# A 1-core f32 transformer pair: GpSimd exchanges halves for the rotary step, modulation rows go through memory, and experts are chosen in three groups of tiles with X spilled

## Chip, cores, metric

One Trainium2 chip, one core. The metric is the device time of one execution in microseconds. Three runs of the kernel before took 1822.27, 1818.64 and 1820.02 us: median 1820.02. The profiled execution took 1820.39 us; its first to last instruction, the span, is 1819.1 us.

## What is computed

Two transformer blocks in f32 on 512 tokens of width 1024. The first block is a hybrid mixer (differential attention with rotary queries and keys beside an mLSTM), a cross attention over 256 memory rows, and a mixture of 32 experts; the second runs two layers of a convolution beside a sparse attention, each behind a modulated norm. What the change touches, cut from the reference:

```python
def rotary(t, pos):                       # per head of 64: halves of 32
    t1, t2 = t[..., : d // 2], t[..., d // 2:]
    return jnp.concatenate([t1 * cos - t2 * sin, t2 * cos + t1 * sin], axis=-1)

x = x + cross_attention(rms_norm(x, norm_x_g), rms_norm(mem, norm_mem_g), w_xq, w_xk, w_xv, w_xo)
x = x + hierarchical_moe(rms_norm(x, norm_ffn_g), w_rg, b_rg, w_re, b_re, w1, w3, w2)
# in hierarchical_moe
g_idx = jnp.argmax(softmax(xt @ w_rg + b_rg))                 # one of 4 groups
e_logits = (xt @ w_re + b_re) of that group                   # 8 experts, the best 2 are taken
y = (silu(x_blk @ w1[e]) * (x_blk @ w3[e])) @ w2[e]           # rows sorted by expert
# in the second block, for each of two layers
mod = silu(c) @ w_ada[l] + b_ada[l]; shift, scale, gate = split(mod, 3)
h = rmsnorm(x, g_pre[l]) * (1 + scale) + shift
```

## The kernel before

Every engine runs its own program, written out by hand in the order of its work. `Count.step` adds to a semaphore when an instruction ends, `done` gives the value to wait for. The kernel is walked twice, once to number the steps and once to build. PSUM is eight banks of 128 x 512, handed out in turn by `Banks.take`: TensorE waits for whoever last read the bank. SBUF is one arena. Weights of 2 MB each go through ring slots (`Ring`): SP issues a load when the last reader of its slot is done (`ends`; the issue is line 164), so the order of loads and the time at which slots come free set the weight stream. `product` (line 185, its matmul is line 187) is the helper through which nearly all products go; each 128x128 by 128x512 f32 product of one chunk is two matmul instructions, so a product over 8 chunks is sixteen.

**Input stage** (`pe_mixer_in`, `act_mixer_in`, `dve_mixer_in`). For each of 8 groups g of queries and keys TensorE makes a product "qk"; ACT copies it to `raw[g % 2]`; TensorE multiplies `raw` by a permutation matrix (`pe_swap`, line 614), which exchanges the halves of 32 within each 64 partitions; DVE multiplies the exchanged rows by a signed sine (line 1249), `raw` by the cosine (1250), and adds them (1252). `raw` is free again when the rotation two groups back is done. Between rotations DVE sums w_ada's rows weighted by silu(c) into `macc` (`dve_ada`, lines 1211 and 1214: one multiplication and seven multiply-adds of 512 columns for each half). When both halves of a part (shift or scale) are in, TensorE sums over the partitions (`pe_mod`, line 576): eight products of 128x128 by a column of ones, so that the 1024 sums stand as [128, 8], and DVE adds the bias (`dve_mod`). For layer 0 the two sums stand behind "qk" 4 and 6. Then come four value products, and attention. For layer 1 the two sums stand in the output projection of the mixer, behind its fourth and its last tile, ahead of the transposes of the normalised rows for cross attention.

**Router** (`pe_router`, `act_router`, `dve_router`). The last projection w_xo is made in eight products of tile t and half n. For each of four tiles DVE adds it to X (line 1460), ACT sums squares, GpSimd takes the root (line 1763), DVE makes the normalised row times the gain (`dve_put_f`, line 1494), ACT stores the row to memory (`h3_rows`), and TensorE transposes it (line 801). Logits are made for two tiles at a time, turned back to tokens (821), and picked on DVE (`dve_router_pick`, lines 1555 to 1589: a chain of some 20 small operations); ranks, places and the table of slots follow (`dve_router_place`, lines 1600 to 1605, and 1631 to 1634). With the table GpSimd gathers the rows of each expert by indirect DMA (line 1776), once h3 is all stored.

**Experts.** 32 experts with w1, w3 and w2 of 2 MB each, 96 loads in the order w1.0 w3.0 w1.1 w3.1 w2.0 w1.2 w3.2 w2.1 ... (w2 of an expert follows w1 and w3 of the next). Nine slots take them in turn; the first ones are loaded while cross attention and router still run, the two that held w_xo when it is done, `features` (HT) when the logits are done, and `router` when slots and stores are done. For each expert TensorE turns 64 gathered rows (875), multiplies by w1 and w3 side by side, turns (898), multiplies by w2; ACT and DVE copy, and GpSimd scatters the result (1784). Behind the experts the scattered rows are read back and added to X (`dve_row_sum`, `pe_row_sum`).

## Time and profile before

| | |
|---|---|
| median of 3 runs | 1820.02 us |
| profiled execution, device time | 1820.39 us |
| its span | 1819.1 us |
| PE busy | 1653.1 us, 91% of the span |
| DVE, ACT, POOL busy | 727.4, 478.0, 317.5 us |
| DMA | 324.30 MB, 178 GB/s over the span |
| expert weights | 96 loads of 2 MB, median 34.7 us from issue to landing |

A line of code named in the profile is a line of the kernel before; a line can be that of a helper. PE is TensorE, PEld its weight loads, DVE VectorE, ACT ScalarE, POOL GpSimd, SP SyncE. PEclk is the granted clock of TensorE, as a share of 2.4 GHz; the DMA share is the mean busy share of the 16 DMA engines. "<-" names what ended an engine's idle time. A row of a timeline that merges instructions ("x88") names the form of the first.

### The profile page before, as it was taken

To read this page: it belongs to the slowest core of one execution; us is meant where nothing else is said; L and a number is where in the kernel's file an instruction comes from. 1 tells how busy PE (TensorE), PEld (TensorE's weight loads), DVE (VectorE), ACT (ScalarE), POOL (GpSimd) and SP (SyncE) were. 2 spreads that over 40 slices of the span, in tenths; PEclk is the share of its full clock that TensorE was granted. 3 is DMA by queue.
4 is the path that set the end of the run, shared out by engine and by line. 5 is a ranking of instruction groups with operands and counts; after the bars stand their busy time and mean duration, and the time that the engine had idled before them with its cause. 6 is when DMAs were issued, how large, how long until landed. Compare 5 with 4: busy or idle time off the path is not lost.

```text
span 1819.1 us, 15312 instructions
## 1 busy us (share of the span) xinstructions
PE 1653.1 (91%) x5832; PEld 814.8 (45%) x5832; DVE 727.4 (40%) x1519; ACT 478.0 (26%) x979; POOL 317.5 (17%) x312
## 2 busy tenths in 40 slices
PE   6999999999989699898887787999989999998898
PEld 3544446645454333333333333444455554445553
DVE  2626634254152312111100111459875143996622
ACT  2013242101130010000000001566365134645631
POOL 0000000000000112111101100148143012742500
PEclk9899999999999799898898998989999999899999
DMA  8321032356262599999999998401102130020101
GB/s 322 139 93 46 1 116 93 139 185 236 69 248 87 220 365 408 407 401 409 402 399 403 407 415 325 178 1 70 69 1 88 46 110 0 7 109 24 47 1 46
DMA packets 70960, 324.30 MB, mean 178 GB/s; under 512 B 9290, under 2 KB 12626, under 8 KB 58464
## 3 DMA queue, kind: packets, MB, share of 16 engines
q1 hardware_dynamic: 63552, 308.03, 43.6%
q0 software_dynamic: 6016, 10.51, 1.8%
q10 hardware_dynamic: 1312, 4.72, 0.7%
q8 instruction: 48, 0.79, 0.2%
q14 instruction: 32, 0.26, 0.0%
HBM read 318.95 MB, written 12.67 MB: 182 GB/s over the span
## 4 chain that ended last, share of the span: by engine, by line
PE 68%; DMA 19%; DVE 9%; ACT 2%; issue 2%; POOL 0%; SPq 0%; ACTq 0%; DVEq 0%; POOLq 0%
PE bank L187 65%; DMA arena<-in_w 15%; DMA arena<-h_rows,arena 3%; DVE arena L2454 1%; DVE arena L1214 1%; DVE arena L2438 1%; PE bank L2053 1%; PE bank L567 1%; DVE arena L2495 1%; DVE arena L2508 0%; PE bank L875 0%; DMA arena<-in_params 0%; PE bank L2000 0%; PE bank L662 0%; DVE bank L2486 0%
## 5 line engine op out<-in xcount | busy, mean ns | idle before, releaser
L187 PE MATMUL bank<-arena 128*128 128x512 f32 (+11 forms) x4964 | 1548.0, 551 | 90.6 <-DMA arena<-in_w 53.2
L187 PEld LDWEIGHTS bank<-arena 128*128 128x128 f32 (+3 forms) x4964 | 710.4, 181 | 858.9 <-issue 789.5
L2669 POOL TENSOR_TENSOR arena<-arena 128x512 f32<-128x512 f32 x180 | 205.4, 1141 | 224.1 <-ACT arena L2279 206.6
L1763 POOL TENSOR_TENSOR arena<-arena 128x1 f32<-128x1 f32 (+2 forms) x44 | 32.4, 738 | 682.3 <-DVE arena L1204 456.9
L1711 DVE TENSOR_TENSOR arena<-arena,bank 64x512 f32<-64x512 f32 x32 | 22.1, 691 | 314.2 <-ACT arena L1170 314.2
L2279 ACT ACTIVATE arena<-arena 128x512 f32<-128x512 f32 x180 | 125.9, 717 | 19.6 <-POOL arena L2669 19.3
L959 ACT COPY arena<-bank 128x512 f32<-128x512 f32 (+3 forms) x114 | 60.8, 540 | 228.4 <-PE bank L187 147.3
L1170 ACT ACTIVATE arena<-bank 64x512 f32<-64x512 f32 x32 | 18.9, 591 | 379.6 <-PE bank L187 379.6
L1784 POOL DMA_INDIRECT y_rows<-arena x32 | 32.1, 1004 | 413.4 <-PE bank L875 272.6
L1705 DVE COPY arena<-bank 128x512 f32<-128x512 f32 x32 | 22.1, 692 | 115.2 <-PE bank L875 115.2
L1214 DVE SCALAR_TENSOR_TENSOR arena<-arena 128x512 f32<-128x512 f32 x84 | 63.2, 752 | 3.0
L2466 DVE MAX8 arena<-arena 128x8 f32<-128x512 f32 (+2 forms) x96 | 54.1, 563 | 3.3
L2438 DVE SCALAR_TENSOR_TENSOR arena<-arena 128x512 f32<-128x512 f32 x60 | 54.6, 910 | 0.9
L875 PE MATMUL bank<-arena 64*128 64x64 f32 x256 | 35.0, 281 | 22.0 <-DMA arena<-h_rows,arena 22.0
L2053 PE MATMUL bank<-arena 128*128 128x128 f32 x160 | 27.2, 290 | 27.6 <-DVE arena L2508 19.4
L2468 DVE MATCH_REPLACE8 arena<-arena 128x512 f32<-128x512 f32 (+2 forms) x96 | 52.2, 544 | 0.0
L875 PEld LDWEIGHTS bank<-arena 64*128 64x128 f32 x256 | 30.6, 200 | 47.0 <-DMA arena<-h_rows,arena 30.8
L2454 DVE SCALAR_TENSOR_TENSOR arena<-arena 128x512 f32<-128x512 f32 (+2 forms) x42 | 42.7, 1017 | 4.5 <-ACT arena L2226 0.2
L2241 ACT ACTIVATE arena<-arena 128x128 f32<-128x128 f32 (+3 forms) x64 | 35.5, 555 | 33.8 <-DVE arena L2495 23.3
L2486 DVE TENSOR_TENSOR bank<-bank,arena 128x256 f32<-128x256 f32 (+1 forms) x44 | 22.0, 499 | 55.7 <-PE bank L187 55.6
L1180 ACT COPY arena<-bank 128x512 f32<-128x512 f32 x32 | 18.8, 586 | 92.4 <-PE bank L187 92.4
L2053 PEld LDWEIGHTS bank<-arena 128*128 128x128 f32 x160 | 18.7, 145 | 51.3 <-DVE arena L2508 33.6
(264 smaller groups left out, 876.6 us busy)
## 6 DMA issues: line engine op xcount, KB each, us to landing
arena<-in_w SPq DMA_DIRECT2D x96, 2048.0 KB, 34.7
arena<-in_w_in SPq DMA_DIRECT2D x15, 2048.0 KB, 10.8
arena<-in_w_ada SPq DMA_DIRECT2D x12, 2048.0 KB, 8.7
arena<-in_w_out SPq DMA_DIRECT2D x6, 2048.0 KB, 7.7
arena<-in_w_xk SPq DMA_DIRECT2D x2, 2048.0 KB, 9.3
arena<-in_w_xv SPq DMA_DIRECT2D x2, 2048.0 KB, 8.6
arena<-in_w_xq SPq DMA_DIRECT2D x2, 2048.0 KB, 9.9
arena<-in_w_xo SPq DMA_DIRECT2D x2, 2048.0 KB, 9.1
```

Source lines behind the costliest of these rows:

```text
L187: i = pe.e.matmul(o, l, r, start=first and j == 0, stop=last and j == len(pairs) - 1)
L875: i = pe.e.transpose(b[:, c * BLK:(c + 1) * BLK], xg[:, c, :], k.ident[0:BLK, 0:BLK])
L959: act.e.copy(dst, src).then_inc(*k.act.step(*name))
L1214: dve.e.scalar_tensor_tensor(out=acc, in0=w[:, c, :], scalar=k.CACT[:, c:c + 1], in1=acc, op0=ALU.mult, op1=ALU.add).then_inc(*(k.dve.step ...
L2053: i = pe.e.transpose(b[:, c * 128:(c + 1) * 128], k.tmp[s % 4][:, c * 128:(c + 1) * 128], k.ident)
L2241: i = act.e.activation(e, e, ACT.Exp, scale=-1.0 if g == 1 else 1.0, bias=ds[:, j:j + 1], accum_out=ds[:, 4 + j:5 + j])
L2279: act.e.activation(k.prod[l][n % 4], x, ACT.Identity, scale=w, bias=0.0).then_inc(*k.act.step("prod", l, f, j))
L2438: dve.e.scalar_tensor_tensor(out=yc, in0=x, scalar=cw, in1=yc, op0=ALU.mult, op1=ALU.add).then_inc(*V.step("tap", l, f, j))
L2454: dve.e.scalar_tensor_tensor(out=S, in0=r, scalar=w, in1=S, op0=ALU.mult, op1=ALU.add).then_inc(*V.step("is", l, n))
L2466: dve.e.max(m8, S).then_inc(*V.step())
L2468: dve.e.match_replace(S, m8, S, TAKEN).then_inc(*V.step())
L2669: pool.e.tensor_tensor(yc, yc, k.prod[l][n % 4], ALU.add).then_inc(*k.pool.step("sum", l, f, j))
```

## The change

1. *Exchange on GpSimd.* `pe_swap` and its matrix go. Behind ACT's copy of group g, GpSimd makes four multiplications of 32 partitions by 512, each reading one quadrant of `raw` and of the sine (its rows exchanged beforehand) and writing the neighbouring quadrant of `rt[g % 2]`. DVE's sine multiplication goes; it waits for GpSimd, multiplies by the cosine and adds.
2. *Shift and scale as rows.* The sum over partitions is now a product of a column of ones by 256 columns of `macc`, four of them into partitions 0, 32, 64 and 96 of the bank. DVE copies it to `mrow`, ACT issues four stores to memory, GpSimd one load that brings it back as [128, 8]; bias, 1 and gain are put in by DVE ahead of the experts.
3. *Router.* Tiles are chosen in groups (0, 1), (2), (3). TensorE transposes X itself, by chunks of 128 columns, half a tile at a time; the gain is multiplied into the router's weights, the root into the logits. Logits of two chunks are made side by side in 64 columns each and added in the turn back. Tile 3 of the last projection is split in halves, with the router's steps of the first groups between. The stored row is X times its root, made by ACT; the gain is multiplied in when an expert's rows are copied.
4. *X in memory.* ACT stores X, its 2 MB of SBUF become a tenth slot, and SP loads X back behind the last expert weight. SP waits for the last stored row ahead of w3 of expert 2, and for both first gathers ahead of w2 of expert 1.

The diff, cut to its core:

```diff
-        slots = [i * 4096 for i in range(SLOTS)] + [base + 5876, base + 9972, ht_at, base + 14068]
+        slots = [i * 4096 for i in range(SLOTS)] + [base + 5876, base + 9972, ht_at, base + 14068, x_at]
...
-    R.ends[features] = [(P, ("lg", 1))]
+    R.ends[features] = [(P, ("lg", 2))]
     R.ends[router] = [(P, ("slot",)), (k.h3_out[0], ("h3", 2)), (k.h3_out[1], ("h3", 3))]
-    R.go_on([ring[2], ring[3], tokens, cross, ring[4], ring[0], ring[1], features, router])
+    R.ends[residual] = [(k.x_out, ("x", 3)), (k.act, ("sq", "f", 3)), (k.act, ("xn", "f", 3)), (P, ("tr", 3, 1))]
+    R.go_on([ring[2], ring[3], tokens, cross, ring[4], ring[0], ring[1], features, residual, router])
     def expert(name, e, c, n, end):
         R.load(sp, (name, e), k.a[name][e].rearrange("(p c) n -> p c n", c=c), (c, n), P, (end, e))
...
     for e in range(NE + 1):
         if e < NE:
             expert("w1", e, 8, 512, "up")
+            if e == 2:
+                sp.wait_ge(*k.h3_out[1].done("h3", 3))
             expert("w3", e, 8, 512, "up")
+            if e == 2:
+                for j in range(2):
+                    sp.wait_ge(*k.xg_in[j].done(j))
             if e == 0:
                 sp.wait_ge(*P.done("xs", 7))
-                sp.e.dma_start(k.WR, rows(k.a["w_router"], 8, 40)).then_inc(*k.wr_in.step("w"))
+                sp.e.dma_start(k.WR, chunks(k.a["w_router"], 8)).then_inc(*k.wr_in.step("w"))
         if e:
             expert("w2", e - 1, 4, 1024, "dn")
+    for c, n in R.ends[residual]:
+        sp.wait_ge(*c.done(*n))
+    sp.e.dma_start(k.X, k.x_d.rearrange("(t p) d -> p t d", p=128)).then_inc(*k.x_back.step("x"))
...
-    acc = k.macc.rearrange("p (q k) -> p k q", k=8)
     pe.wait_ge(*k.dve.done("ada", l, part, 1))
-    for c in range(8):
-        i = product(pe, b[:, c:c + 1], [(acc[:, c, :], k.C("ones", 0, 1))])
+    for n in range(4):
+        i = product(pe, b[32 * n:32 * n + 1, 0:256], [(k.C("ones", 0, 1), k.macc[:, n * 256:(n + 1) * 256])])
     i.then_inc(*k.pe.step("mod", l, part))
...
-        if g:
-            pe_swap(k, pe, g - 1)
...
-def pe_swap(k, pe, g):
-    b = k.banks.take(pe, k.dve, "swap", g)
-    pe.wait_ge(*k.act.done("qk", g))
-    product(pe, b, [(k.C("swap"), k.raw[g % 2])]).then_inc(*k.pe.step("swap", g))
...
+GROUPS = ((0, 1), (2,), (3,))
+def pe_router_turn(k, pe, t, halves=(0, 1)):
+    for q in halves:
         b = k.banks.take(pe, k.dve if q else k.act, "tr", t, q, among=ROUTER_BANKS)
-        pe.wait_ge(*k.dve.done("xn", "f", t))
+        pe.wait_ge(*k.dve.done("o", "w_xo", t, q))
         for f in range(4):
-            i = pe.e.transpose(b[:, f * 128:(f + 1) * 128],
-                               k.XNf[t % 2].rearrange("p (q k) -> p k q", k=8)[:, 4 * q + f, :], k.ident)
+            i = pe.e.transpose(b[:, f * 128:(f + 1) * 128], k.X[:, t, q * 512 + f * 128:q * 512 + f * 128 + 128], k.ident)
         i.then_inc(*k.pe.step("tr", t, q))
-def pe_router_logits(k, pe, u):
-
-    w = k.WR
-    pe.wait_ge(*k.wr_in.done("w"))
-    b = k.banks.take(pe, k.act, "lg", u, among=ROUTER_BANKS)
-    for t in (2 * u, 2 * u + 1):
-        pe.wait_ge(*k.act.done("tr", t, 0))
-        pe.wait_ge(*k.dve.done("tr", t, 1))
-    product(pe, b[0:40, 0:256], [(w[:, c, :], k.HT[:, c, u * 256:u * 256 + 256]) for c in range(8)]).then_inc(*k.pe.step("lg", u))
+def pe_router_out(k, pe, t, n, half):
+    b = k.banks.at("o", "w_xo", t, n) if half else k.banks.take(pe, k.dve, "o", "w_xo", t, n, among=ROUTER_BANKS)
+    w = k.ring.at(("w_xo", half), 4, 1024)
+    i = product(pe, b, [(k.OT[:, 4 * half + c, t * 128:(t + 1) * 128], w[:, c, n * 512:(n + 1) * 512]) for c in range(4)],
+                not half, bool(half))
+    if half:
+        i.then_inc(*k.pe.step("o", "w_xo", t, n))
+def pe_router_logits(k, pe, u, pairs, first=True, last=True):
+    t, end = GROUPS[u][0], GROUPS[u][-1] + 1
+    cols = slice(t * 128, end * 128)
+    n = (end - t) * 128
+    pe.wait_ge(*k.dve.done("wr"))
+    b = k.banks.take(pe, k.act, "lg", u, among=ROUTER_BANKS) if first else k.banks.at("lg", u)
+    for j, pair in enumerate(pairs):
+        for m, c in enumerate(pair):
+            pe.wait_ge(*(k.act.done("tr", end - 1, 0) if c < 4 else k.dve.done("tr", end - 1, 1)))
+            i = product(pe, b[64 * m:64 * m + 64, 0:n], [(k.WR[:, c, :], k.HT[:, c, cols])],
+                        first and j == 0, last and j == len(pairs) - 1)
+    if last:
+        i.then_inc(*k.pe.step("lg", u))
...
-    pe_out(k, pe, "w_xo", k.OT, [(2, 1), (3, 0)])
+    pe_out(k, pe, "w_xo", k.OT, [(2, 1)])
+    pe_router_logits(k, pe, 0, [(c, c + 4) for c in range(4)])
+    pe_router_out(k, pe, 3, 0, 0)
+    pe_router_tokens(k, pe, 0)
     pe_router_turn(k, pe, 2)
-    pe_out(k, pe, "w_xo", k.OT, [(3, 1)])
-    pe_router_logits(k, pe, 0)
-    pe_router_tokens(k, pe, 0)
-    pe_router_turn(k, pe, 3)
-    pe_router_logits(k, pe, 1)
+    pe_router_out(k, pe, 3, 0, 1)
+    pe_router_ranks(k, pe, 0)
+    pe_router_logits(k, pe, 1, [(c, c + 4) for c in range(4)])
+    pe_router_out(k, pe, 3, 1, 0)
     pe_router_tokens(k, pe, 1)
-    pe_router_ranks(k, pe, 0)
+    pe_router_turn(k, pe, 3, (0,))
+    pe_router_out(k, pe, 3, 1, 1)
     pe_router_slots(k, pe, 0)
     pe_router_ranks(k, pe, 1)
+    pe_router_logits(k, pe, 2, [(0, 1), (2, 3)], True, False)
+    pe_router_turn(k, pe, 3, (1,))
+    pe_router_logits(k, pe, 2, [(4, 5), (6, 7)], False, True)
+    pe_router_tokens(k, pe, 2)
     pe_router_slots(k, pe, 1)
+    pe_router_ranks(k, pe, 2)
+    pe_router_slots(k, pe, 2)
...
+        if g in (5, 7):
+            act_mod(k, act, 0, g // 2 - 2)
...
+    act.wait_ge(*k.pool.done("root", "f", t))
+    act.e.activation(k.XNf[t % 2], k.X[:, t, :], ACT.Copy, scale=k.f_ss[:, t:t + 1]).then_inc(*k.act.step("xn", "f", t))
+    act.wait_ge(*k.act.last())
     act.e.dma_start(k.h3_d[t * 128:(t + 1) * 128, :], k.XNf[t % 2]).then_inc(*k.h3_out[t % 2].step("h3", t))
+def act_router_squares(k, act, t):
+    act.wait_ge(*k.dve.done("o", "w_xo", t, 1))
+    if t >= 2:
+        act.wait_ge(*k.h3_out[t % 2].done("h3", t - 2))
+    act.e.activation(k.XNf[t % 2], k.X[:, t, :], ACT.Square, accum_out=k.f_ss[:, t:t + 1]).then_inc(*k.act.step("sq", "f", t))
...
+    for t in range(3):
+        act_router_squares(k, act, t)
+        if t == 2:
+            act_router_logits(k, act, 0)
+        act_router_turn(k, act, t)
+        act_x_store(k, act, t)
+        act_row_store(k, act, t)
+    act_router_logits(k, act, 1)
     act_router_turn(k, act, 3)
-    act_router_logits(k, act, 1)
+    act_router_squares(k, act, 3)
+    act_router_logits(k, act, 2)
+    act_row_store(k, act, 3)
+    act_x_store(k, act, 3)
...
+    if (l, part) != (0, 0):
+        dve.wait_ge(*k.mod_out.done((2 * l + part - 1) // 2, (part + 1) % 2, 3))
     dve.wait_ge(*k.pe.done("mod", l, part))
-    if part == 0:
-        dve.e.tensor_tensor(dst, b[:, 0:8], k.P(f"bshift{l}"), ALU.add).then_inc(*V.step("mod", l, part))
-    else:
-        dve.e.tensor_tensor(dst, b[:, 0:8], k.P(f"bscale{l}"), ALU.add).then_inc(*V.step("mod", l, part))
-        dve.wait_ge(*V.last())
-        dve.e.tensor_scalar(dst, dst, 1.0, None, ALU.add).then_inc(*V.step())
-        dve.wait_ge(*V.last())
-        dve.e.tensor_tensor(dst, dst, k.P(f"gpre{l}"), ALU.mult).then_inc(*V.step("scale", l))
+    dve.e.tensor_copy(k.mrow[0:97, :], k.banks.at("mod", l, part)[0:97, 0:256]).then_inc(*k.dve.step("mod", l, part))
+def act_mod(k, act, l, part):
+    act.wait_ge(*k.dve.done("mod", l, part))
+    for n in range(4):
+        act.e.dma_start(k.mod_d[2 * l + part:2 * l + part + 1, n * 256:(n + 1) * 256],
+                        k.mrow[32 * n:32 * n + 1, :]).then_inc(*k.mod_out.step(l, part, n))
+def pool_mod(k, pool, l, part):
+    pool.wait_ge(*k.mod_out.done(l, part, 3))
+    pool.e.dma_start(k.MOD[:, 2 * l + part, :], k.mod_d[2 * l + part].rearrange("(p k) -> p k", k=8)).then_inc(
+        *k.mod_in.step(l, part))
+def dve_mod_end(k, dve, l):
+    V, shift, scale = k.dve, k.MOD[:, 2 * l, :], k.MOD[:, 2 * l + 1, :]
+    dve.wait_ge(*k.mod_in.done(l, 1))
+    dve.e.tensor_tensor(shift, shift, k.P(f"bshift{l}"), ALU.add).then_inc(*V.step("shift", l))
+    dve.e.tensor_tensor(scale, scale, k.P(f"bscale{l}"), ALU.add).then_inc(*V.step())
+    dve.wait_ge(*V.last())
+    dve.e.tensor_scalar(scale, scale, 1.0, None, ALU.add).then_inc(*V.step())
...
-        dve.wait_ge(*P.done("swap", g))
-        dve.e.tensor_tensor(tmp, B.at("swap", g), C("sin"), ALU.mult).then_inc(*V.step("swap", g))
+        dve.wait_ge(*k.pool.done("swap", g))
         dve.e.tensor_tensor(raw, raw, C("cos"), ALU.mult).then_inc(*V.step())
         dve.wait_ge(*V.last())
...
+def pool_swap(k, pool, g):
+    raw, tmp = k.raw[g % 2], k.rt[g % 2]
+    pool.wait_ge(*k.act.done("qk", g))
+    if g >= 2:
+        pool.wait_ge(*k.dve.done("rot", g - 2))
+    for q in range(4):
+        src, dst = slice(32 * q, 32 * q + 32), slice(32 * (q ^ 1), 32 * (q ^ 1) + 32)
+        i = pool.e.tensor_tensor(tmp[dst, :], raw[src, :], k.C("sin")[src, :], ALU.mult)
+    i.then_inc(*k.pool.step("swap", g))
...
+    for t in range(3):
         dve_add_out(k, dve, "w_xo", t)
         dve_mean_square(k, dve, k.f_ss[:, t:t + 1], D, "f", t)
-        if t == 2:
-            dve_gate(k, dve, 1, 1)
-        dve_put_f(k, dve, t)
-        if t < 3:
+        if t < 2:
             dve_router_turn(k, dve, t)
+    dve_gate(k, dve, 1, 1)
     dve.e.memset(k.TAB, 2 * T).then_inc(*V.step("tab"))
-    dve_router_pick(k, dve, 0, lambda: dve_router_turn(k, dve, 3))
+    dve_router_pick(k, dve, 0, lambda: dve_router_turn(k, dve, 2))
+    dve_add_half(k, dve, "w_xo", 3, 0)
     dve_router_place(k, dve, 0)
     dve_router_pick(k, dve, 1)
+    dve_add_half(k, dve, "w_xo", 3, 1)
+    dve_router_turn(k, dve, 3)
+    dve_mean_square(k, dve, k.f_ss[:, 3:4], D, "f", 3)
     dve_router_place(k, dve, 1)
+    dve_router_pick(k, dve, 2)
+    dve_router_place(k, dve, 2)
...
-    dve.e.tensor_copy(k.xt[e % 2], B.at("xT", e).rearrange("p (k s) -> p k s", k=8)).then_inc(*V.step("xT", e))
+    dve.e.tensor_tensor(k.xt[e % 2], B.at("xT", e).rearrange("p (k s) -> p k s", k=8),
+                        k.P("gffn").unsqueeze(2).broadcast_to([128, 8, BLK]), ALU.mult).then_inc(*V.step("xT", e))
...
+    pool.wait_ge(*k.c2_in.done("consts"))
+    for g in range(8):
+        pool_swap(k, pool, g)
+    for part in range(2):
+        pool_mod(k, pool, 0, part)
```

## Rows read from the trace of the kernel before

**Rows 1.** The page: PE busy time, and the chain by engine

```profile
PE 1653.1 (91%) x5832; PEld 814.8 (45%) x5832; DVE 727.4 (40%) x1519; ACT 478.0 (26%) x979; POOL 317.5 (17%) x312
...
PE 68%; DMA 19%; DVE 9%; ACT 2%; issue 2%; POOL 0%; SPq 0%; ACTq 0%; DVEq 0%; POOLq 0%
```

**Rows 2.** Busy us (x instructions), PEclk, DMA share and GB/s by stage

```profile
0.00:123.00 123.00, 108.55 (x272) 53.72 (x272) 47.15 (x78) 15.48 (x24) 2.39 (x8) 0.96 0.51 187
...
598.00:642.00 44.00, 26.68 (x128) 15.20 (x126) 16.70 (x71) 5.50 (x9) 6.19 (x7) 0.77 0.63 232
642.00:1107.00 465.00, 398.25 (x1796) 161.24 (x1796) 58.62 (x122) 37.52 (x64) 64.94 (x66) 0.90 1.01 406
```

**Rows 3.** Timeline of the input stage: start us, us, engine, line, instructions

```profile
20.09 38.08 PE L187 MATMUL bank<-arena 128*128 128x512 f32 x88 [0.89 <-ACT arena L952]
58.54 22.62 PE L187 MATMUL bank<-arena 128*128 128x1 f32 x52 [0.37 <-DVE arena L1214]
81.44 57.79 PE L187 MATMUL bank<-arena 128*128 128x1 f32 x160 [0.28 <-DVE arena L1214]
...
123.31 0.58 ACT L959 COPY arena<-bank 128x512 f32<-128x512 f32 x1 [13.15 <-PE bank L187]
```

**Rows 4.** Window right behind the second summing product of the input stage

```profile
85.50:89.00 3.50, 3.50 (x5) 1.37 (x5) 0.45 (x3) 0.00 (x0) 0.00 (x0) 0.52 0.00 0
```

**Rows 5.** Groups: gate product, DVE accumulation and rotation, GpSimd addition (its ns min/median/max)

```profile
L187 PE MATMUL bank<-arena 128*4 128x512 f32 x32 | 7.0, 591 | 0.0
...
L1214 DVE SCALAR_TENSOR_TENSOR arena<-arena 128x512 f32<-128x512 f32 x84 | 63.2, 752 | 3.0
...
L1252 DVE TENSOR_TENSOR arena<-arena 128x512 f32<-128x512 f32 x8 | 5.5, 694 | 0.3
...
L2669 POOL TENSOR_TENSOR arena<-arena x180: 1087/1090/1570, 1198.4 to 1724.7; 128x512 f32<-128x512 f32 x180
```

**Rows 6.** Timeline of DVE and GpSimd where both run at once

```profile
1203.33 8.48 DVE L2454 SCALAR_TENSOR_TENSOR arena<-arena 128x512 f32<-128x512 f32 x7
...
1203.65 1.38 POOL L2669 TENSOR_TENSOR arena<-arena 128x512 f32<-128x512 f32 x1 [0.71 <-ACT arena L2279]
...
1208.45 1.09 POOL L2669 TENSOR_TENSOR arena<-arena 128x512 f32<-128x512 f32 x1 [0.43 <-ACT arena L2279]
```

**Rows 7.** Window behind an idle stretch of PE that ended at 509.8 us

```profile
510.00:515.00 5.00, 5.00 (x17) 4.17 (x17) 1.56 (x6) 1.49 (x5) 0.00 (x0) 0.50 1.02 429
```

**Rows 8.** Timeline at the first output projection, and one DMA issue of ACT

```profile
368.88 65.83 PE L187 MATMUL bank<-arena 128*128 128x512 f32 x160 [2.40 <-DVE arena L1452]
...
434.35 0.75 DVE L1485 TENSOR_SCALAR arena<-arena 128x1024 f32<-128x1024 f32 x1 [0.44 <-POOL arena L1763]
...
L1116 ACTq DMA_DIRECT2D h_rows<-arena x4: 326/330/333, 569.4 to 602.8; - x4
```

**Rows 9.** Timeline of the router: one pick of two tiles, slots, gather, landing

```profile
598.80 0.69 DVE L1460 TENSOR_TENSOR arena<-arena,bank 128x512 f32<-128x512 f32 x1 [5.58 <-PE bank L187]
...
611.95 0.23 DVE L1555 TENSOR_TENSOR arena<-bank,arena 128x80 f32<-128x80 f32 x1
...
616.01 0.23 DVE L1581 TENSOR_TENSOR arena<-arena 128x64 f32<-128x64 f32 x1
...
620.79 0.18 DVE L1631 TENSOR_SCALAR arena<-bank 64x32 f32<-64x32 f32 x1 [2.01 <-PE bank L187]
...
622.05 1.04 POOL L1776 DMA_INDIRECT arena<-h_rows,arena  x1 [18.77 <-DVE arena L1634]
...
630.02 2.02 PE L875 MATMUL bank<-arena 64*128 64x64 f32 x16 [7.98 <-DMA arena<-h_rows,arena]
```

**Rows 10.** Windows around the expert stage, and the issues of its weights

```profile
630.00:642.00 12.00, 11.67 (x56) 5.60 (x56) 2.31 (x6) 1.28 (x2) 1.86 (x2) 0.78 0.18 40
...
1120.00:1130.00 10.00, 4.21 (x16) 1.37 (x12) 0.00 (x0) 0.59 (x1) 1.47 (x2) 0.83 0.35 123
...
arena<-in_w SPq DMA_DIRECT2D x96, 2048.0 KB, 34.7
```

183 lines of the change are left out of this document (92 added, 91 removed).

## The prediction

> **What bounds the kernel now.** I read the page first: PE is busy nine tenths of the span and holds 68% of the chain, DMA 19% [rows 1]. Then the windows by stage: up to 598 us PE has little idle time, from 598 to 642 it is idle 17 us, and from 642 to 1107 the DMA share is 1.01 at 406 GB/s [rows 2]. So three things are to be priced: PE's work in the input stage, the latency of the router, and the moment from which the weight stream runs without a gap. Behind 1131 us the change alters nothing that I can price, and I let it stand.
>
> **Input stage, PE.** 88 instructions take 38.08 us, 0.433 each [rows 3], so a product of sixteen takes 6.9 and an exchange product of two 0.87. From 20.1 to the end of the last value product at about 122.7 (ACT copies it at 123.3, rows 3) are 102.6 us: twelve products 83.1, eight exchanges 6.9, and 12.6 for the two sums over partitions (pe_mod). These cost 6.3 each because their sixteen one-column instructions take about 4 and because PE then runs at 1.2 GHz: the granted clock behind the second is 0.52 for 3.5 us [rows 4]. The exchanges go. A sum becomes eight instructions of 256 columns into four column groups; the nearest row is the gate product, 32 instructions of 512 columns in 7.0 us as pairs [rows 5], so 0.11 each for half the columns, 0.9 in all. Bounds: 0.5 if four run at once, 1.7 if none do. I take 1.0. If PE never waited, the stage would end at 20.1 + 83.1 + 2.0 = 105.2, 17.5 sooner.
>
> **Input stage, GpSimd and DVE.** It will wait. The exchange becomes four GpSimd multiplications of 32 partitions and 512 columns. The trace has none of that form; the nearest is the addition of 128 partitions, 1.09 at the median [rows 5], and I take that, since a partition holds as many elements. Bounds: 0.3 (the four side by side) and 1.6 (about the longest of that row, 1.57). DVE loses one of three operations a rotation, and its accumulations for the sums have two SBUF inputs. Seven such took 8.48 us while four GpSimd additions began [rows 6], against 0.752 each alone [rows 5]: 3.2 more, 0.8 for each GpSimd operation. The chain: the second product ends at 34.0, ACT copies it (0.6), GpSimd 4.4, DVE rotates (1.4 with 0.69 an operation, rows 5): 40.4. Two accumulations of 6.0 and one rotation of 1.3 follow before the first sum: 53.7 undisturbed, under PE's own 54.7. But the exchanges of products 2, 3 and 4 fall in there, 12 operations, 9.6 us: 63.4. PE waits 8.7. Then a copy (0.4), two rotations and two accumulations, 15.0, with seven GpSimd operations, 5.6, put the second sum at 84.0, where PE could be at 78.2. One sum, one query or key product and four value products later it is 119.7, 3.0 sooner than before. After such waits the clock drops: in 510 to 515 us, behind 3.7 us of idleness, it was 0.50 [rows 7]. The first drop hides in the wait for the second sum; the second costs about 2. **Gain 1.0.** GpSimd's own queue has nothing else to do meanwhile, the DMA issues of the rows (four on ACT, 0.33 each, one on GpSimd) stand beside PE work, and the rotation of the last key product is done by 98, before attention wants it. The Trainium skill ("SBUF — State Buffer", Within the engine side) says that such a pair holds the port exclusively for the whole instruction: a GpSimd operation would then cost DVE 1.09 and not 0.8, the 19 of them 5.5 us more, and the sum would be 1815. The row shows a part overlapped, and I keep to the row.
>
> **Output projection.** The 160 instructions take 65.83 [rows 8]; 128 are projection, 55.4, so the two sums cost 5.2 each. The first falls to 1.0: 4.2. The second covers DVE's chain to the last normalised tile, which ends at 435.1 [rows 8], four us behind the last projection; without the cover PE waits for it: 0. ACT's four issues, 0.33 each [rows 8], now stand before its first copy of features: up to 1.3 lost, I take 0.5. **Gain 3.7.**
>
> **Router.** Before: the last projection ends 0.6 before DVE's addition at 598.8, slots at 620.8, gather issued 622.05, landed 630.02 [rows 9]. After, on the same clock: transposes of X itself need no root and no gain, and logits, ranks and picks of the first tiles lie between halves of the last projection. They push that one back by 6.7, to 604.9. A pick took 4.1 for two tiles [rows 9], 3.1 for one. Behind the last projection come addition and transposes with the slots of the first group (2.8), copy, logits, copy, turn back (2.3), one pick (3.1), ranks, place, slots and index (2.2): 615.3, and the gather is issued 0.9 later at 616.2, 5.8 sooner. Three small groups instead of two cost DVE one more pick, hidden under the projection. Landing took 8.0 with one weight load in flight; now w3 of expert 2 is in flight, but issued 2 us before, behind the last stored row: 6.4, so 622.6, **7.4 sooner**. Bounds: issue 3 to 8 sooner, landing 4 to 8.
>
> **Weight stream.** Before, from 630 to 642 the DMA share is 0.18, since all nine slots are full until expert 0's first half is done; from 642 on 87 loads take 465 us, 5.35 each [rows 2, 10]. After, SP holds w2 of expert 1 until both gathers have landed. Seven loads are in; 89 remain, of which three have free slots (X's is one), 16 us, longer than expert 0's first half needs. So the stream has no gap from 624.6 on and ends at 624.6 + 476 = 1100.4: **gain 6.8**. The stores of X, 2 MB, lie in the projection's idle DMA time except the last. X comes back behind the last weight: 2.1 MB, 5.2 us at the stream's rate; from 1120 to 1130 the DMA share is 0.35 [rows 10], which hides it, but the last scatter meets it: 0 to 5, I take **1.0 lost**. Eight small DVE operations for shift and scale, about 1.6, and the gain multiplied in at each expert's copy hide under expert 0's weights.
>
> **Sum.** 1.0 + 3.7 + 6.8 − 1.0 = 10.5. The profiled execution is 1820.4 (span 1819.1), 0.4 above the median: **1810**.
>
> **Rivals.**
> (B) The four GpSimd multiplications run side by side, a swap taking some 1.3 instead of 4.4. Then DVE meets the first sum in time, PE waits 3 at the second, and the stage ends at 108.0, 14.7 sooner and not 1.0: 1796. For it: they use different partitions and nothing waits between them. Against: no row shows GpSimd operations overlapping. The Trainium skill ("GPSIMD Engine Reference", the note on consecutive Pool instructions) has each core go on to the next instruction once its own 16 partitions are done, which is this case. Chance 0.27.
> (C) The gather lands no sooner, because GpSimd also waits for the last stored row, whose store stands last on ACT. Then the stream starts at 632 and ends 0.6 later than before, plus 1.0 for X: 1817. For it: ACT does the scaled copy only after the last logits. Against: that copy ends at 611, five us before the gather's issue. Chance 0.10.
> (D) Slower: reading one quadrant and writing another makes the multiplication dearer. At 1.6 with the same overlap, 19 of them hold DVE back 9.7 more, and two exchanges that stand alone ahead of a rotation 2 each; the stage ends some 13.5 later than forecast: 1823. It decides from about 1.5 an operation. For it: the form is in no row. Against: the element count is that of the 1.09 row. Chance 0.10.
> The forecast has 0.50; 0.03 is left for what I have not seen.
>
> **How the numbers follow.** A measurement of this kernel can tell about 0.2%, 3.6 us, from no change. Forecast and B lie below 1816.4, C about on the bound (half of it same), D above. Faster 0.82, same 0.08, slower 0.10. The forecast's own range is 1803 to 1816 by its bounds; with B the range reaches down to 1792, and up to 1819 for C; D and the rest, 0.13, are outside.
>
> **What would show it.** Value products ending near 122 with PE idle before both sums (forecast) or near 108 without the first (B); GpSimd multiplications of 1.1 us in a row, not at once; DVE's accumulations there at up to 1.5 us instead of 0.75; no clock drop behind the sums themselves. In the router a gather issued 11 us behind the last projection and not 24, and no gap of the DMA share between the gather's landing and the last weight. The forecast is wrong in its largest term if the accumulations stay at 0.75, and in its second if the stream has a gap or ends less than 480 us behind the landing.

## The result, and the profile after

The changed kernel took 1807.16 us (median of 5 runs, 1802.55 to 1809.38) beside 1819.09 us before (5 runs, 1817.05 to 1822.27): ratio 0.9931, 95% interval 0.9917 to 0.9944, so it is faster by more than the noise. The forecast was 1810, with a range of 1803 to 1816. The profiled execution is the one of 1807.16 us, with a span of 1805.8, 13.3 less than in the profile before.

The page of the changed kernel: busy time, the chain by engine, and the groups of DVE's accumulations and GpSimd's multiplications (busy us, mean ns, idle before):

```profile
PE 1629.6 (90%) x5808; PEld 795.6 (44%) x5808; DVE 738.5 (41%) x1525; ACT 483.4 (27%) x984; POOL 366.5 (20%) x348
...
PE 66%; DMA 20%; DVE 10%; ACT 2%; issue 1%; POOL 1%; DVEq 0%; ACTq 0%; POOLq 0%; SPq 0%
...
L1264 DVE SCALAR_TENSOR_TENSOR arena<-arena 128x512 f32<-128x512 f32 x84 | 78.4, 934 | 3.0
...
L1349 POOL TENSOR_TENSOR arena<-arena 32x512 f32<-32x512 f32 x32 | 46.4, 1449 | 41.5 <-ACT arena L999 38.5
```

The windows by stage of the changed kernel, columns as in [rows 2]:

```profile
0.00:123.00 123.00, 94.04 (x244) 43.05 (x244) 60.64 (x68) 15.75 (x25) 50.08 (x42) 0.94 0.51 187
598.00:642.00 44.00, 32.60 (x176) 17.25 (x176) 13.81 (x56) 8.39 (x12) 6.76 (x8) 0.81 0.88 337
642.00:1107.00 465.00, 401.39 (x1788) 163.55 (x1786) 57.37 (x120) 35.37 (x60) 64.81 (x67) 0.90 1.00 405
```

PE is 14.5 us less busy in the first stage and the stage is as long as before. Between 598 and 642 us the DMA share is 0.88 where it was 0.63 [rows 2].

To see where the 13.3 us come from, one takes the same events in both timelines. Five of the kernel before that [rows 3, 8, 9] do not hold: the first product of cross attention, of w_xo, of expert 31, the last product of expert 31, and the first product of the second block.

```profile
442.11 64.03 PE L187 MATMUL bank<-arena 128*128 128x512 f32 x164 [0.15 <-issue]
...
540.05 20.84 PE L187 MATMUL bank<-arena 128*128 128x512 f32 x48 [0.87 <-DVE arena L1502]
...
1107.57 10.54 PE L187 MATMUL bank<-arena 128*64 128x512 f32 x48 [2.46 <-DMA arena<-in_w]
...
1119.33 3.65 PE L187 MATMUL bank<-arena 128*64 128x512 f32 x16 [0.61 <-DVE arena L1719]
1127.75 1.22 PE L187 MATMUL bank<-arena 128*128 128x256 f32 x2 [4.76 <-issue]
```

The timeline of the changed kernel behind the input stage: the output projection with PE's waits behind it, the same events, DVE's last addition of the projection w_xo, and the gather:

```profile
373.53 56.48 PE L187 MATMUL bank<-arena 128*128 128x512 f32 x144 [2.40 <-DVE arena L1532]
...
432.29 0.38 PE L581 MATMUL bank<-arena 128*128 128x128 f32 x1 [1.85 <-DVE arena L1569]
433.48 5.33 PE L581 MATMUL bank<-arena 128*128 128x128 f32 x29 [0.82 <-DVE arena L1569]
...
439.71 64.02 PE L187 MATMUL bank<-arena 128*128 128x512 f32 x164 [0.15 <-issue]
...
534.77 20.84 PE L187 MATMUL bank<-arena 128*128 128x512 f32 x48 [0.87 <-DVE arena L1576]
...
599.35 0.69 DVE L1539 TENSOR_TENSOR arena<-arena,bank 128x512 f32<-128x512 f32 x1 [0.45 <-PE bank L187]
...
611.47 1.04 POOL L1864 DMA_INDIRECT arena<-h_rows,arena  x1 [6.52 <-DVE arena L1719]
...
617.04 2.02 PE L906 MATMUL bank<-arena 64*128 64x64 f32 x16 [5.58 <-DMA arena<-h_rows,arena]
...
1094.58 10.54 PE L187 MATMUL bank<-arena 128*64 128x512 f32 x48 [2.59 <-DMA arena<-in_w]
...
1106.35 3.65 PE L187 MATMUL bank<-arena 128*64 128x512 f32 x16 [0.61 <-DVE arena L1805]
1115.45 7.68 PE L187 MATMUL bank<-arena 128*128 128x256 f32 x20 [5.45 <-issue]
```

| event | before | after | gained on the way there |
|---|---|---|---|
| ACT copies the last value tile | 123.31 | 122.73 | 0.6 |
| output projection begins | 368.88 | 373.53 | −5.2 |
| cross attention begins | 442.11 | 439.71 | 7.1 |
| w_xo begins | 540.05 | 534.77 | 2.9 |
| the gathered rows have landed | 630.02 | 617.04 | 7.7 |
| last product of expert 31 | 1119.33 | 1106.35 | 0.0 |
| second block begins | 1127.75 | 1115.45 | −0.7 |
| end of the span | 1819.1 | 1805.8 | 1.0 |

**Input stage.** The changed kernel's timeline there (PE's products; GpSimd's exchanges of the first and the third group; DVE's seven multiply-adds of each half; ACT's last copy):

```profile
20.03 34.64 PE L187 MATMUL bank<-arena 128*128 128x512 f32 x80 [0.89 <-ACT arena L983]
65.61 16.03 PE L187 MATMUL bank<-arena 128*1 128x256 f32 x40 [10.94 <-DVE arena L1264]
86.06 39.31 PE L187 MATMUL bank<-arena 128*1 128x256 f32 x102 [4.42 <-DVE arena L1264]
...
27.93 5.21 POOL L1349 TENSOR_TENSOR arena<-arena 32x512 f32<-32x512 f32 x4 [14.66 <-ACT arena L999]
...
41.62 6.35 POOL L1349 TENSOR_TENSOR arena<-arena 32x512 f32<-32x512 f32 x4 [1.66 <-ACT arena L999]
...
41.85 11.84 DVE L1264 SCALAR_TENSOR_TENSOR arena<-arena 128x512 f32<-128x512 f32 x7
...
56.53 9.03 DVE L1264 SCALAR_TENSOR_TENSOR arena<-arena 128x512 f32<-128x512 f32 x7
...
67.65 5.47 DVE L1264 SCALAR_TENSOR_TENSOR arena<-arena 128x512 f32<-128x512 f32 x7
...
122.73 0.59 ACT L990 COPY arena<-bank 128x512 f32<-128x512 f32 x1 [13.15 <-PE bank L187]
```

PE waits 10.94 and 4.42 us for DVE in front of the two sums. The seven multiply-adds took 5.47 us where GpSimd was idle and 11.84 where it ran all but half a microsecond. The four multiplications took 5.21 us alone, 1.30 each, one behind the other.

**Attention, whose code is unchanged.** It came out 5.2 us longer. The granted clock behind three short pauses of PE, before (first three rows) and after (last three):

```profile
183.00:187.00 4.00, 2.38 (x14) 1.59 (x13) 3.89 (x7) 2.38 (x6) 0.00 (x0) 1.00 0.03 6
206.00:210.00 4.00, 4.00 (x13) 1.80 (x14) 3.86 (x10) 0.70 (x3) 0.00 (x0) 1.00 0.00 0
236.00:240.00 4.00, 4.00 (x14) 1.93 (x13) 2.98 (x10) 1.82 (x5) 0.00 (x0) 1.00 0.55 167
```

```profile
184.00:188.00 4.00, 3.46 (x11) 2.52 (x12) 3.86 (x8) 1.27 (x5) 0.00 (x0) 0.59 0.00 0
208.00:212.00 4.00, 4.00 (x9) 1.89 (x9) 3.86 (x10) 0.63 (x2) 0.00 (x0) 0.58 0.00 0
238.00:242.00 4.00, 3.64 (x8) 1.88 (x9) 3.43 (x11) 2.53 (x9) 0.00 (x0) 0.67 0.26 77
```

The same 22 instructions, before and after:

```profile
207.15 7.69 PE L187 MATMUL bank<-arena 128*128 128x128 f32 x22
```

```profile
208.47 9.38 PE L187 MATMUL bank<-arena 128*128 128x128 f32 x22
```

The pauses are the same ones (1.25, 0.90 and 0.90 us); before, TensorE stayed at 2.4 GHz behind them; after, it fell to 1.2 GHz for a while (the windows' 0.58 to 0.67 mix both levels; in windows of 2 us the granted clock was 0.50 from 186, 210 and 240 us on), 1.7 us dearer for the 22 instructions shown. I call this a low spell. After the change there are three more of them in attention. There are two fewer in the output projection (before, the clock was 0.50 in 370 to 372 and in 404 to 406 us), a shorter one behind it, and none behind PE's pause of 3.7 us ahead of 507.4, where the clock before the change was 0.50 [rows 7].

### The profile page after: what moved, and what is told of

Its sections match the earlier page's. It is cut to its first block, busy times and chain, and to the rows that moved or that the text cites. A ratio compares the mean times of both kernels' runs of the same rounds, so it can differ in the third digit from the quotient of the medians.

```text
span 1805.8 us, 15346 instructions
## 1 busy us (share of the span) xinstructions
PE 1629.6 (90%) x5808; PEld 795.6 (44%) x5808; DVE 738.5 (41%) x1525; ACT 483.4 (27%) x984; POOL 366.5 (20%) x348
## 4 chain that ended last, share of the span: by engine, by line
PE 66%; DMA 20%; DVE 10%; ACT 2%; issue 1%; POOL 1%; DVEq 0%; ACTq 0%; POOLq 0%; SPq 0%
PE bank L187 62%; DMA arena<-in_w 15%; DMA arena<-h_rows,arena 3%; DVE arena L1264 2%; DVE arena L2551 1%; PE bank L2149 1%; DVE arena L2535 1%; PE bank L581 1%; POOL arena L1349 1%; DVE arena L2605 1%; DVE arena L2592 1%; DMA arena<-in_w_ada 0%; DMA arena<-in_params 0%; PE bank L666 0%; PE bank L906 0%
## 5 line engine op out<-in xcount | busy, mean ns | idle before, releaser
L187 PE MATMUL bank<-arena 128*128 128x512 f32 (+11 forms) x4944 | 1525.5, 551 | 100.4 <-DMA arena<-in_w 49.8
L187 PEld LDWEIGHTS bank<-arena 128*128 128x128 f32 (+5 forms) x4944 | 692.8, 178 | 865.6 <-issue 788.0
L1264 DVE SCALAR_TENSOR_TENSOR arena<-arena 128x512 f32<-128x512 f32 x84 | 78.4, 934 | 3.0
L1790 DVE TENSOR_TENSOR arena<-bank,arena 128x512 f32<-128x512 f32 x32 | 22.1, 692 | 112.0 <-PE bank L906 111.9
L1349 POOL TENSOR_TENSOR arena<-arena 32x512 f32<-32x512 f32 x32 | 46.4, 1449 | 41.5 <-ACT arena L999 38.5
L2535 DVE SCALAR_TENSOR_TENSOR arena<-arena 128x512 f32<-128x512 f32 x60 | 53.0, 883 | 0.9
```

The lines of the kernel that those rows point to most:

```text
L187: i = pe.e.matmul(o, l, r, start=first and j == 0, stop=last and j == len(pairs) - 1)
L1264: dve.e.scalar_tensor_tensor(out=acc, in0=w[:, c, :], scalar=k.CACT[:, c:c + 1], in1=acc, op0=ALU.mult, op1=ALU.add).then_inc(*(k.dve.step ...
L1349: i = pool.e.tensor_tensor(tmp[dst, :], raw[src, :], k.C("sin")[src, :], ALU.mult)
L2535: dve.e.scalar_tensor_tensor(out=yc, in0=x, scalar=cw, in1=yc, op0=ALU.mult, op1=ALU.add).then_inc(*V.step("tap", l, f, j))
```

## Experiments

The theory from the two profiles: (1) the input stage gained nothing because GpSimd's operations hold DVE back and PE waits for DVE at two fixed places; (2) the sums as rows are worth about as much as their PE time at full clock; (3) the router is worth what the gather lands sooner; (4) holding loads back for the gather and the tenth slot nearly cancel. Low spells add a few microseconds either way. All times below are medians; the kernel before, run beside each group, took 1819.9 us (e1 to e4), 1820.9 (e5 to e8), 1821.6 (e9 to e11) and 1820.7 (e12).

### e1: the exchange back on TensorE

```diff
-        dve.wait_ge(*k.pool.done("swap", g))
+        dve.wait_ge(*P.done("swap", g))
+        dve.e.tensor_tensor(tmp, B.at("swap", g), C("sin"), ALU.mult).then_inc(*V.step("swap", g))
...
+        if g:
+            pe_swap(k, pe, g - 1)
```

> The changed kernel with the exchange of halves back on PE (eight products with the swap matrix, DVE's multiplication by the sine as before); rows sums, router and spilled X stay. Theory A (GpSimd's multiplications hold DVE back, and PE waits for DVE's accumulations): no GpSimd operation is left beside DVE, the accumulations fall from a mean of 1297 ns in the input stage back to about 752, PE waits at most 3 us in front of the two sums instead of 15.4, pays 6.9 for the eight products, and the value products end near 112 to 114 instead of 122.1; time about 1798 to 1800. Rival B (PE would wait at the sums whatever GpSimd does, because DVE's own accumulations are late or their weights land late): the waits stay over 10 us and the 6.9 us of products are added: 1814. A clock spell more or less in attention (each costs 1 to 2 us) is noise on both.

Measured: 1794.59 us (1790.63 to 1798.3), ratio 0.9851 (0.9838 to 0.9863), 12.6 us better than the whole change. PE's two sums in its timeline, and DVE's accumulations in the stage's groups:

```profile
59.71 16.29 PE L187 MATMUL bank<-arena 128*1 128x256 f32 x44 [0.37 <-DVE arena L1279]
76.28 52.84 PE L187 MATMUL bank<-arena 128*1 128x256 f32 x152 [0.28 <-DVE arena L1279]
```

```profile
L1279 DVE SCALAR_TENSOR_TENSOR arena<-arena 128x512 f32<-128x512 f32 x28 | 21.0, 752 | 1.0
```

The accumulations are back at 752 ns (1297 in the changed kernel's stage), the waits are 0.65 us instead of 15.4, and the last value tile is copied 91.9 us behind the stage's first product instead of 102.7. Theory A holds: the exchange on GpSimd made the stage 10.8 us longer although it freed PE of 6.9. The median lies 3.4 below the 1798 expected, and why is not shown: the profiled execution is the slowest of the five (1798.3). In it the stretch from the last value tile to w_xo took 408.5 us, against 412.0 in the changed kernel and 416.7 before, with fewer low spells, and the stretch from the head of the second block to the end took 3.5 longer than in the changed kernel.

### e2: sums by columns, e3: the router part alone

e2 puts `pe_mod` and `dve_mod` back as they were, with GpSimd still exchanging; e3 takes e1 and e2 together, which leaves of the change only router, stream and spilled X.

```diff
-    for n in range(4):
-        i = product(pe, b[32 * n:32 * n + 1, 0:256], [(k.C("ones", 0, 1), k.macc[:, n * 256:(n + 1) * 256])])
+    for c in range(8):
+        i = product(pe, b[:, c:c + 1], [(acc[:, c, :], k.C("ones", 0, 1))])
```

> The changed kernel with the four sums as before (sixteen one-column instructions each, DVE adds shift and scale at once, no rows through memory); GpSimd keeps the exchange. Theory A (the sums cost 4 us of PE time each, and the clock falls behind them): the output projection with its sums takes some 5 us more (65 instead of 60), and the input stage 3 to 6 more, since PE's first and second sum stand behind DVE in the chain and only clock already lost to the waits is not lost again; 1815 to 1818. Rival B (the sums' PE time is hidden where PE waits anyway, and ACT's and GpSimd's issues of the rows cost as much as they save): within 2 us of the changed kernel, 1807 to 1809.

> The kernel before with the router part and the spilled X alone: exchange on PE and one-column sums as before. Theory A (router and stream are worth 7.7 us less 1 for X): about 1819.1 - 6.7 = 1812 to 1813, gather landing 7 to 8 us sooner behind the first w_xo product than before. Rival B (a large part of the router's gain in the profile comes from the earlier arrival or from a clock spell): 1815 to 1818.

Measured: e2 1815.42 us (9 runs, 1814.58 to 1817.9), ratio 0.9974 (0.9964 to 0.9984), 8.3 more than the change; e3 1815.06 us (6 runs, 1813.17 to 1815.15), ratio 0.9967 (0.9955 to 0.9979). The output projection of e2, and the last expert of e3:

```profile
375.01 62.44 PE L187 MATMUL bank<-arena 128*128 128x512 f32 x160 [2.39 <-DVE arena L1534]
```

```profile
1101.50 13.49 PE L187 MATMUL bank<-arena 128*64 128x512 f32 x48 [2.45 <-DMA arena<-in_w]
```

e2: the projection and its two sums took 62.44 us here and 56.48 in the changed kernel, so a sum by rows takes 3.0 less than one by columns (the granted clock was 1.00 in both stretches); but behind them the changed kernel waits 1.85 and 0.82 for the last normalised tile, so cross attention begins 66.2 us behind the projection's start instead of 68.9: 2.7 gained. In the kernel before the same 160 instructions took 65.83 [rows 8]; the 3.4 beyond e2's are low spells. The input stage took 5.9 longer with the sums by columns (108.6 behind its first product). 2.7 and 5.9 make 8.6, against 8.3 between the medians.

e3 comes out at rival B's figure, though only partly for its reason: the gather lands 82.7 us behind w_xo's first product, 7.3 sooner than before (90.0) as theory A has it; 1.4 are lost on the way to w_xo, and 3.0 in the last expert, whose 48 instructions took 13.49 instead of 10.54 us in a low spell (clock 0.50 from 1101 to 1105 us). The profile wins 2.2 back in the second block, for no reason that the change gives.

### e4: the exchange on ACT

ACT copies each quadrant of the PSUM bank to its neighbour's place, then DVE multiplies by the sine in SBUF.

```diff
+        for q in range(4):
+            act.e.activation(k.rt[g % 2][32 * (q ^ 1):32 * (q ^ 1) + 32, :], B.at("qk", g)[32 * q:32 * q + 32, :],
+                             ACT.Copy, scale=0.125 if g < 4 else 1.0)
...
-        dve.wait_ge(*k.pool.done("swap", g))
+        dve.wait_ge(*A.done("qk", g))
+        dve.e.tensor_tensor(tmp, tmp, C("sin"), ALU.mult).then_inc(*V.step("swap", g))
```

> The changed kernel with the exchange on ACT: four copies of 32 partitions from the PSUM bank into the exchanged places, then DVE multiplies by the sine in SBUF; no GpSimd operation and no PE product. Theory A (what hurts in the changed kernel is GpSimd beside DVE, not the route of the exchange): PE pays nothing for the exchange, DVE's operations are at their undisturbed length, PE waits some 5 us for the two sums in all, the value products end at 107 to 110: 1794 to 1797, 2 to 5 better than the exchange on PE. Rival B (ACT's five operations a product, some 3 us, hold back DVE's chain and the banks): PE waits as long as before, 1800 to 1807.

Measured: 1788.85 us (1786.87 to 1793.11), ratio 0.983 (0.9818 to 0.9843), 18.3 better than the change. PE's products and ACT's four copies:

```profile
20.88 49.14 PE L187 MATMUL bank<-arena 128*128 128x512 f32 x120 [0.89 <-ACT arena L983]
...
70.45 51.13 PE L187 MATMUL bank<-arena 128*1 128x256 f32 x148 [0.42 <-DVE arena L1267]
```

```profile
28.04 2.39 ACT L1000 ACTIVATE arena<-bank 32x512 f32<-32x512 f32 x4 [7.76 <-PE bank L187]
```

PE goes through the stage with one wait of 0.42 us, 84.8 from its first product to the last copy. It is better than theory A allowed (some 5 us of waiting). A likely reason, from the order of the program and not tested by itself, is that DVE can rotate as soon as ACT has copied, not one product later as with TensorE's exchange.

### e10 and e11: what a GpSimd operation costs

e10 has one multiplication of 128 partitions where the change has four of 32; e11 has four, each written to the quadrant that it reads. Both leave out the exchange of halves.

```diff
-    for q in range(4):
-        src, dst = slice(32 * q, 32 * q + 32), slice(32 * (q ^ 1), 32 * (q ^ 1) + 32)
-        i = pool.e.tensor_tensor(tmp[dst, :], raw[src, :], k.C("sin")[src, :], ALU.mult)
+    i = pool.e.tensor_tensor(tmp, raw, k.C("sin"), ALU.mult)
```

> The changed kernel with one GpSimd multiplication of 128 partitions by 512 for each query and key product in place of four of 32 partitions; the halves are not exchanged, so this leaves the exchange out. Theory A (a GpSimd operation takes a time by its elements in a partition, whatever the number of partitions): each takes 1.1 to 1.4 us, as long as one of the four did, so GpSimd's work falls to a quarter, DVE's accumulations fall to a mean below 900 ns, PE waits less than 2 us before the sums, and the value products end near 106 to 108: 1790 to 1794. Rival B (GpSimd's time goes by all elements, so one whole operation takes what the four took): about 4 us each and the stage as in the changed kernel, 1805 to 1808.

> The changed kernel with its four GpSimd multiplications of 32 partitions, each written to the partitions that it reads; the halves are not exchanged, so this leaves the exchange out. If writing to another quadrant makes the operation dearer (as rival D of the prediction had it), an undisturbed one takes 1.1 instead of 1.30 us and the stage ends 3 to 5 us sooner: 1802 to 1804. If the crossing costs nothing, the operations take 1.30 us and the time is that of the changed kernel within its scatter, 1804 to 1809.

Measured: e10 1791.52 us (4 runs, 1790.54 to 1799.42), ratio 0.9843 (0.9814 to 0.9873); e11 1810.51 us (4 runs, 1806.55 to 1811.29), ratio 0.9929 (0.9905 to 0.9953). GpSimd's multiplications, three of e10 in its timeline, then four of e11:

```profile
29.01 1.26 POOL L1347 TENSOR_TENSOR arena<-arena 128x512 f32<-128x512 f32 x1 [15.74 <-ACT arena L999]
35.83 1.27 POOL L1347 TENSOR_TENSOR arena<-arena 128x512 f32<-128x512 f32 x1 [5.55 <-ACT arena L999]
42.71 1.31 POOL L1347 TENSOR_TENSOR arena<-arena 128x512 f32<-128x512 f32 x1 [5.61 <-ACT arena L999]
```

```profile
28.37 5.22 POOL L1349 TENSOR_TENSOR arena<-arena 32x512 f32<-32x512 f32 x4 [14.92 <-ACT arena L999]
```

A multiplication of 512 columns takes 1.3 us, with 32 partitions or with 128, across quadrants or straight. Splitting it in four is most of the price: in e10 DVE's multiply-adds take 882 ns instead of 1297, PE waits 2.68 us at the sums, and the last copy comes 88.7 behind the first product instead of 102.7 (84.8 in e4, with no GpSimd operation). Crossing costs nothing that shows: four multiplications take 5.22 us straight and 5.21 across, and e11's ratio is 0.9929 where the changed kernel's is 0.9931.

### e12: GpSimd's exchange kept, the sums later

```diff
-        if g == 4:
+        if g == 6:
             pe_mod(k, pe, 0, 0)
-        elif g == 6:
-            pe_mod(k, pe, 0, 1)
...
         pe_by_token(k, pe, ("v", t), A if t % 2 else V, R.at(("w_in", 2), 8, 512), t)
+        if t == 1:
+            pe_mod(k, pe, 0, 1)
```

> The changed kernel, the exchange left on GpSimd, with its two sums of the input stage later in PE's order: the first behind the seventh query or key product instead of the fifth, the second behind the second value product instead of the seventh query or key product. Theory A (PE loses only what it waits for at the sums; DVE and GpSimd have the time once the sums are later): the first accumulations are ready at 65.5 as now and PE comes at 68.6, the second at about 88 and PE comes at 90, PE waits less than 2 us in all instead of 15.4, and the value products end 83 to 86 us behind the stage's first product instead of 102.7: 1789 to 1793. Rival B (the work held back turns up as a wait further on, by the rotation of the last keys or by the banks): the stage's gain is given back in part by a wait of PE before or in attention, 1796 to 1805.

Measured: 1787.58 us (5 runs, 1784.94 to 1788.11), ratio 0.9814 (0.9793 to 0.9835), 19.6 better than the change and a little below the range expected. Its last value tile is copied at 104.98, 84.3 us behind the first product. Its input stage on PE, and DVE's accumulations there:

```profile
20.71 100.19 PE L187 MATMUL bank<-arena 128*128 128x512 f32 x268 [0.89 <-ACT arena L983]
```

```profile
L1264 DVE SCALAR_TENSOR_TENSOR arena<-arena 128x512 f32<-128x512 f32 x28 | 36.3, 1298 | 1.0
```

DVE is held back as much as in the changed kernel (1298 ns a multiply-add), and PE does not wait once in 100 us: what was lost was lost by where PE asked for the sums.

### e5 to e9: holds and tenth slot

e5 takes away SP's two waits in the stream, e6 keeps them and leaves X in SBUF (nine slots), e7 does both, e8 and e9 are e4's exchange without both waits and without the second alone.

```diff
-            if e == 2:
-                sp.wait_ge(*k.h3_out[1].done("h3", 3))
...
-            if e == 2:
-                for j in range(2):
-                    sp.wait_ge(*k.xg_in[j].done(j))
```

> The changed kernel without SP's two waits in the weight stream (for the last stored rows before w3 of expert 2, for both first gathers before w2 of expert 1); ten slots as before. Theory A (the stream is the bound from the gather on, and what counts is how many loads are left when it runs without a gap): the gather lands 1 to 2 us later because more loads are in flight, the ten slots are full before it, the stream stands until expert 0's first half is done some 12 us after the landing, and then 86 loads of 5.35 take 460: w3 of expert 31 is used 472 us behind the landing instead of 477.5; in sum 3 to 4 faster, 1803 to 1804. Rival B (the holds are what brings the gather 7.7 us sooner): it lands 3 to 8 us later, and the time is 1807 to 1810.

> The changed kernel with X kept in SBUF (nine slots for the experts' weights, no stores of X and no load back); SP's two waits stay. Theory A (with the waits only seven loads are in before the gather, two free slots are 10.7 us of loads, about as long as expert 0's first half, so the tenth slot buys nothing, and X's 4 MB are only a cost behind the last weight): w3 of expert 31 is used 477 to 479 us behind the landing as now, the head of the second block comes up to 1 us sooner: 1806 to 1808. Rival B (the tenth slot is what closes the gap): a gap of 2 to 5 us in the DMA share behind the landing, 1809 to 1812.

> Nine slots and no waits of SP in the stream: the stream as it was before the change, under the new router. Theory A: landing 1 to 2 us later than in the changed kernel, a gap as before, 477.5 us from landing to w3 of expert 31, X's return saved: 1807 to 1809. Rival B (the holds or the tenth slot carry much of the router's gain): 1811 or more.

> The exchange on ACT together with a stream without SP's two waits, ten slots. If the two effects add (theory A of both): 1788.9 - 3.5 = 1785 to 1786. If the holds are what brings the gather early (rival): 1789 to 1792.

> The exchange on ACT; of SP's two waits only the one for the last stored rows (before w3 of expert 2) stays, the one for both gathers (before w2 of expert 1) goes. Theory (the first wait is what lets GpSimd issue the gather at once instead of 5 to 6 us later; the second only keeps three loads back while the DMA engines are idle): the gather is issued as early as with both waits, lands 0 to 2 us later than then, and the stream behind it is some 4 us shorter: 1784 to 1786, and 0 to 3 better than without both. Rival (the second wait is what makes the gather land early, and without it the gather queues behind three loads of 5.35): landing 5 to 10 us later: 1788 to 1793.

Measured, with the ratio's interval. "Ready" is the start of PE's last product of the router, which waits for the same DVE operation as the gather; "landed" PE's first product with gathered rows (in e9 those of expert 0 alone, expert 1's were used 3.1 us later; in the others both were in); "last" the last product of expert 31:

| kernel | us | interval | ready to landed | landed to last | both |
|---|---|---|---|---|---|
| before | 1819.1 | | 8.6 | 489.3 | 497.9 |
| the change: ten slots, both waits | 1807.2 | 0.9917 to 0.9944 | 6.2 | 489.3 | 495.5 |
| e6: nine slots, both waits | 1806.3 | 0.9901 to 0.9936 | 6.6 | 488.7 | 495.2 |
| e5: ten slots, no wait | 1804.2 | 0.9905 to 0.9941 | 9.5 | 485.2 | 494.7 |
| e7: nine slots, no wait | 1814.0 | 0.9946 to 0.9974 | 14.2 | 489.1 | 503.3 |
| e4: ten slots, both waits | 1788.9 | 0.9818 to 0.9843 | 6.8 | 489.7 | 496.5 |
| e8: ten slots, no wait | 1785.9 | 0.9795 to 0.9827 | 10.2 | 484.9 | 495.1 |
| e9: ten slots, first wait | 1788.7 | 0.9785 to 0.983 | 9.9 | 486.0 | 495.9 |

The gather in the timelines of e5 and e7, and in e9's:

```profile
612.00 1.04 POOL L1858 DMA_INDIRECT arena<-h_rows,arena  x1 [11.37 <-DMA h_rows<-arena]
...
615.99 2.03 PE L900 MATMUL bank<-arena 64*128 64x64 f32 x16 [8.86 <-DMA arena<-h_rows,arena]
```

```profile
616.86 1.04 POOL L1852 DMA_INDIRECT arena<-h_rows,arena  x1 [11.32 <-DMA h_rows<-arena]
...
625.64 2.02 PE L896 MATMUL bank<-arena 64*128 64x64 f32 x16 [13.59 <-DMA arena<-h_rows,arena]
```

```profile
592.58 1.04 POOL L1865 DMA_INDIRECT arena<-h_rows,arena  x1 [7.11 <-DVE arena L1720]
...
601.88 1.14 PE L903 MATMUL bank<-arena 64*128 64x64 f32 x8 [9.30 <-DMA arena<-h_rows,arena]
```

Without the first wait GpSimd issues the gather 5.4 to 5.7 us behind "ready", because it waits for the last stored row (the releaser named is the store of h_rows; that weight loads delay the store is inferred); with it, 0.6 behind. Without the second alone (e9) the gather takes 9.3 us to land, against 6.2 in e4, which has both. With ten slots the loads that went ahead then shorten the stream behind the landing by 3.7 to 4.8 us. So with ten slots the waits nearly cancel: the last column differs by 0.8 us for e5 and 1.4 for e8, and the traces show no more. The medians of e5 and e8 are each about 3.0 lower, in or near the ranges of my theories, but my reason covers less than half of it, and the intervals of e5, e8 and e9 overlap those of the kernels with both waits, so that a gain is not shown. e5's profiled execution reached w_xo at 530.45 us, 4.3 before the changed kernel's, in code that is the same for PE up to there. e9 came out in its rival's range, though its gather landed 3.1 us later than e4's and not 5 to 10. With nine slots the waits matter: without them the time goes up by 7.7 us (e7 against e6), and their intervals lie apart. This is rival B's figure for e7. I had expected a return to the old stream, 1 to 2 us; the landing was 14.2 behind "ready" instead (8.6 before the change, with the same slots and no waits), and nothing was gained behind it. Why it is that late was not tried. The tenth slot alone buys nothing while the waits stand (e6).

## Why the prediction was right or wrong

**GpSimd and DVE (right in kind, nearly in size).** I took 1.09 us an operation and 0.8 us of DVE's time for each. Measured: 1.30 alone (the row that I took was of additions in place; whether the operation or the place makes the 0.2 was not tried), and before the first sum DVE lost 9.9 in its accumulations and 1.1 in a rotation for twelve operations, 0.92 each. I had PE waiting 8.7 and 5.8; it waited 10.9 and 4.4. I had DVE ready for the sums at 63.4 and 84.0; it was at 65.5 and just under 86. The gain was 0.6 in place of 1.0. The range that I gave for the operation (0.3 to 1.6) held it, and rival D's price did not come about: crossing quadrants cost nothing that shows (e11), and 1.3 lies below its 1.5.

Rival B failed on its premise, that four operations on different partitions run side by side: four took 5.2 us, one of all partitions 1.3 (e10, e11). The Trainium skill ("GPSIMD Engine Reference", Instruction dispatch, the note on consecutive Pool instructions) lets a core go on once its own 16 partitions are done; whether the cores did so cannot be seen here, but it shortened nothing.

On the rule that I set aside: while both engines ran without a break a pair took 1.65 us (a multiply-add of 1.65 beside a multiplication of 1.62) where alone they take 0.75 and 1.30; DVE paid 0.92 an operation, nearer to my 0.8. The Trainium skill ("SBUF — State Buffer", SBUF: two separate sides) has one block the other for the whole instruction: by that rule, with the measured durations, a pair would take 2.05 and DVE would pay 1.30. The trace agrees that each holds the other up, and not with the whole instruction as the price.

**Output projection (right in kind, the first term too large).** The step that failed is "128 are projection, 55.4, so the two sums cost 5.2 each": the 65.83 of that row held 3.4 us of low spells. At full clock (e2) a sum by columns costs 3.5, half of 62.44 less 55.4, and one by rows 3.0 less. The first sum thus gave 3.0 and not 4.2. The second came out near the 0 that I had put for it: it fell by 3.0 as well, and PE waited 2.7 for the last normalised tile in its place. With 0.6 lost in the transposes behind, this makes 2.7 in place of 3.7. The profile's 7.1 is this and low spells.

**Router (right).** Counted from w_xo's first product, the gather was issued 5.3 us sooner (at 76.7 against 82.0; forecast 5.8) and landed 2.4 sooner behind its issue (5.6 against 8.0; forecast 6.4): 7.7 in all, forecast 7.4. It was issued 12.1 behind DVE's last addition of the projection, where my figures gave 10.7 and the kernel before has 23.3. e3 repeats the gain alone with 7.3. Rival C's mechanism is real, and e5, e7 and e8 show it: GpSimd waits for the last stored row. It is SP's first wait that keeps it away (e9 against e8), which I had not written down as its purpose.

**Weight stream (right).** From landing to expert 31's first product are 477.5 us, forecast 477.8, and 477.6 before (624.6 + 476 is 1100.6 and not the 1100.4 that I wrote, so the forecast should read 478.0; the gain of 6.8 goes with 1100.6): closing the gap behind the landing gives nothing by itself, because exactly the loads held back for it have to come behind. The gain is the landing's 7.7 (forecast 6.8). One of my signs of being wrong was badly set: "less than 480 us behind the landing" holds for my own forecast too, so it could not tell right from wrong.

**Tail.** X's return cost 0.7 in the profile (0.8 to 0.9 against e6, where the second block begins 8.25 behind the last expert instead of 9.10), forecast 1.0.

**Sum.** Forecast 10.5, measured 11.9 between the medians and 13.3 between the profiles. Of the latter 10.3 are the terms of my sum (0.6 + 2.7 + 7.7 − 0.7). That this is so near 10.5 is partly luck, since they miss by −0.4, −1.0, +0.9 and +0.3. The other 3.1 I put down to low spells, which I had priced in the input stage alone: −5.2 in attention, 4.4 in the projection (7.1 − 2.7), 2.9 in cross attention, 1.0 in the second block (there by difference only). They are not a fixed effect of the change: e5, with the same order of PE up to w_xo, was there 4.3 sooner (2.6 in the input stage and 3.2 behind it, less 1.4 by which it began later), while e6, e7 and e11 took 412.0 to 412.1 from the last value tile to w_xo, as the changed kernel did. That PE's long waits make them more frequent further on is suggested by the kernels with fewest waits after the change (from the last value tile to w_xo: 416.7 before, 412.0 after, 408.9 in e5, 408.5 in e1, 409.3 in e12, 406.6 in e4), but e5, which waits as the change does, stands among the low ones; this stays open.

What the prediction did not see is the choice it left: the stage could be 18 us shorter with this very exchange (e12).

## What to carry to other kernels

When work is moved off the bounding engine onto a helper, find the place where the bounding engine next asks for something made beside it, and move that place before anything else: two lines of order were worth 19.6 us here, more than the whole change. Count instructions, not partitions, for GpSimd, and for a small move look at an engine beside which DVE keeps its speed (with ACT exchanging, PE waited 0.4 us in all). And before reading what an operation costs from a row, look whether the clock was full in that row.

## What the hardware showed that I had not expected

- A GpSimd multiplication of 512 f32 columns with both inputs in SBUF took 1.26 to 1.31 us with 128 partitions and 1.30 with 32. ACT's copies from PSUM are alike in this: 2.39 us for four of 32 partitions, 0.60 each, and 0.60 for one of 128.
- Two-input operations of DVE and GpSimd on SBUF that run at once slow each other and end one for one: 0.75 and 1.30 us alone, 1.65 a pair, less than the sum and more than the longer.
- The same short pauses of PE (0.9 and 1.25 us) left TensorE at 2.4 GHz in one execution and at 1.2 GHz in another. Executions of like code reached the same instruction 4.3 us apart.

The fastest version measured is e8 (exchange on ACT, sums as rows, new router, ten slots, no waits of SP): 1785.85 us (1783.16 to 1787.21), ratio 0.9811. e4, e9 and e12 lie within 3 us of it, with overlapping intervals, so the order among the four is not shown. e12's order with e8's stream was not run.
